# Pairing VectorE's maxima and normalisations, and two heads' value products side by side in TensorE's columns, in a transformer block on one core

## What is computed

```python
# dil: three patterns, each a band; mixed by a softmax over their log-denominators
s = einsum(q, k) * scale + bias        # bias from 32 buckets of the distance
s = where(mask, s, -inf);  m = max(s);  p = exp(s - m);  l = sum(p)
o = einsum(p / l, v)
# na: the same softmax over a window of rows and 16 columns, with its own bias
# diff: two maps per head
p = softmax(einsum(q * HD ** -0.5, k));  a = p[0] - lam * p[1];  o = einsum(a, v)
```

## Time and profile before

| | |
|---|---|
| three runs | 4605.14 (4602.17 to 4606.09) us |
| the profiled execution | 4605.48 us |
| its span, first to last instruction | 4603.7 us |
| PE busy | 3929.3 us, 85% |
| VectorE busy | 2265.8 us, 49% |
| ScalarE busy | 1411.2 us, 31% |
| mean granted TensorE clock | 0.936 of full |
| mean DMA traffic | 60 GB/s |

### The profile page before, as it was taken

The page is one execution under the profiler, slowest core; times in us unless marked ns, Lnnn a source line. Parts: engine busy times, 40 slices in busy tenths (PEclk is TensorE's granted clock), DMA queues, the critical chain, the costliest instruction groups (busy, mean ns, idle before and its releaser), DMA issues. The chain is left out here.

```text
span 4603.7 us, 56197 instructions
## 1 busy us (share of the span) xinstructions
PE 3929.3 (85%) x20557; PEld 2962.8 (64%) x20557; DVE 2265.8 (49%) x3881; ACT 1411.2 (31%) x2600; POOL 0.2 (0%) x4
## 2 busy tenths in 40 slices
PE   5987988998689998888698888976999888797888
PEld 3554667876456686666587665864667666575566
DVE  3434335553445525666524666234553666436654
ACT  2322223322223313333312444121332434314432
POOL 0000000000000000000000000000000000000000
PEclk8988999998799999999899999987999999899999
DMA  6333234542100021111021000211112111121112
GB/s 224 116 95 80 80 89 142 164 124 73 33 23 27 25 62 37 27 36 28 23 64 42 24 24 22 66 46 36 30 33 79 43 41 36 46 69 28 33 51 74
DMA packets 504246, 275.37 MB, mean 60 GB/s; under 512 B 56665, under 2 KB 489781, under 8 KB 504094
## 3 DMA queue, kind: packets, MB, share of 16 engines
q1 hardware_dynamic: 483186, 252.08, 19.5%
q10 hardware_dynamic: 20908, 21.26, 1.5%
HBM read 271.08 MB, written 10.32 MB: 61 GB/s over the span
## 5 line engine op out<-in xcount | busy, mean ns | idle before, releaser
L558 PE MATMUL ps<-h_high,w_high 128*128 128x512 f32 (+1 forms) x3512 | 1346.5, 383 | 185.1 <-DVEq L2191 128.9
L558 PE MATMUL ps<-h_low,w_high 128*128 128x512 f32 (+1 forms) x3512 | 1293.4, 368 | 0.0
L558 PE MATMUL ps<-h_high,w_low 128*128 128x512 f32 (+1 forms) x3512 | 1288.0, 367 | 0.0
L558 PEld LDWEIGHTS ps<-h_high,w_high 128*128 128x128 f32 x3512 | 682.7, 194 | 351.3 <-DVEq L2191 136.6
L554 DVE TENSOR_TENSOR w_low<-w_raw,w_high 128x1024 fp32r<-128x1024 f32 x378 | 453.6, 1200 | 625.2 <-ACT w_high L544 603.5
L558 PEld LDWEIGHTS ps<-h_low,w_high 128*128 128x128 f32 x3512 | 682.8, 194 | 107.7 <-issue 11.7
L558 PEld LDWEIGHTS ps<-h_high,w_low 128*128 128x128 f32 x3512 | 681.5, 194 | 109.3
L544 ACT ACTIVATE w_high<-w_raw 128x1024 fp32r<-128x1024 f32 x378 | 392.2, 1039 | 784.5 <-PE ps L558 604.6
L558 PE MATMUL ps<-k_high,q_high 64*128 64x256 f32 (+4 forms) x784 | 194.4, 414 | 255.7 <-ACT probs L777 215.2
L777 ACT ACTIVATE probs<-ps,neg_max 128x768 f32<-128x768 f32 (+2 forms) x368 | 288.4, 784 | 361.1 <-DVE neg_max L802 360.2
L558 PE MATMUL ps<-probsT,v 128*128 128x512 f32 (+4 forms) x800 | 338.4, 565 | 12.7 <-DVE probsT L949 6.7
(11 more groups left out here) (192 smaller groups left out, 4000.8 us busy)
## 6 DMA issues: line engine op xcount, KB each, us to landing
w_raw<-in_w_in SPq DMA_DIRECT2D x444, 256.0 KB, 3.1
y_and_merged<-in_w_mod SPq DMA_DIRECT2D x96, 256.0 KB, 3.1
w_raw<-in_w_branch SPq DMA_DIRECT2D x96, 256.0 KB, 3.0
w_raw<-in_w_up SPq DMA_DIRECT2D x88, 256.0 KB, 4.3
y_and_merged<-in_w_ada SPq DMA_DIRECT2D x64, 256.0 KB, 3.4
w_raw<-in_w_out SPq DMA_DIRECT2D x48, 256.0 KB, 3.0
w_raw<-in_w_down SPq DMA_DIRECT2D x44, 256.0 KB, 2.9
y_and_merged<-in_w_ada SPq DMA_DIRECT2D x4, 2048.0 KB, 21.1
```

Source lines behind the costliest of these rows:

```text
L558: return nc.tensor.matmul(*a, **kw)
```

## The change

dil and na join `TWIN`, so that they take swa's path for the values with 4 chunks of both heads instead of 8 of one head; dil, na and diff join `BOTH_FIRST`. In dil and na the wait of the scores is for `maxed` instead of `exped`. The late modulation moves from bank 7, which the odd chunks now use, to the last 128 columns of bank 1.

```diff
-TWIN = ("swa",)
-BOTH_FIRST = ("swa",)
+TWIN = ("dil", "na", "swa",)
+BOTH_FIRST = ("dil", "na", "diff", "swa",)
...
-    st += [Stage("units", name="dil", nn=5, items=8, chunks=8, **units), Stage("units", name="na", nn=4, items=8, chunks=8, **units)]
+    st += [Stage("units", name="dil", nn=5, items=8, chunks=4, **units), Stage("units", name="na", nn=4, items=8, chunks=4, **units)]
...
             if s["first"]:
-                for j in range(2):
-                    for c in range(4):
-                        res.append(([PF[:, j, qt, 128 * c:128 * c + 128] for qt in range(4)], VB[:, c, 64 * j:64 * j + 64],
-                                    PS[64 * j:64 * j + 64, 5 * 512:6 * 512], c == 0, c == 3))
+                for c in range(4):
+                    res.append([([PF[:, j, qt, 128 * c:128 * c + 128] for qt in range(4)], VB[:, c, 64 * j:64 * j + 64],
+                                 PS[64 * j:64 * j + 64, 5 * 512:6 * 512], c == 0, c == 3) for j in range(2)])
...
                 if group * size >= 2:
-                    key = "exped"
+                    key = "maxed" if s["first"] else "exped"
...
-                    mod_block(pe, s, i, s["nn"], e, 0 if e < 4 else 1, 7)
+                    mod_block(pe, s, i, s["nn"], e, 0 if e < 4 else 1, 1, 384)
...
-                    pe_values(pe, s, t, u, i, 0, side=late_mods(i, (1, 2)), first=1)
+                    pe_twin_values(pe, s, t, u, i, side=late_mods(i, (1, 2)))
...
-                    if s["first"] and c in (2, 4):
-                        act_mod(act, s, i, s["nn"], c // 2, 7)
+                    if c in (1, 3):
+                        act_mod(act, s, i, s["nn"], (c + 1) // 2, 1, 384)
...
-                    evac_pt(act, s, t, u, i, 0, 0, beside(i))
+                    evac_twin(act, s, t, u, i, 0, beside(i))
...
-                evac_pt(dve, s, t, u, i, 0, 1, beside)
+                if s["first"]:
+                    evac_twin(dve, s, t, u, i, 1, beside)
+                else:
+                    evac_pt(dve, s, t, u, i, 0, 1, beside)
```

More of the change, by code:

```diff
@@ L599, in mod_total, with mod_block, act_mod @@
             mm(col, MP[:, :], PICK[:, :], start=True, stop=True).then_inc(S["mod_sum"], 1)
-        def mod_block(pe, s, t, per, off, c, b):
+        def mod_block(pe, s, t, per, off, c, b, at=0):
             kk = plain_slot(s, t, per, off)
             pe_wait_plain(pe, s, t, per, off)
-            mod_parts(bank(b, 128), lambda kc: WN[:, kk, 128 * kc:128 * kc + 128], c).then_inc(s_n, 1)
-        def act_mod(act, s, t, per, off, b):
+            mod_parts(bank(b, 128, at), lambda kc: WN[:, kk, 128 * kc:128 * kc + 128], c).then_inc(s_n, 1)
+        def act_mod(act, s, t, per, off, b, at=0):
             act.wait_ge(s_n, cnt(s, "n", t, per, off + 1))
-            act.activation(MP[:, :], bank(b, 128), ACT.Copy).then_inc(S["mod_copy"], 1)
+            act.activation(MP[:, :], bank(b, 128, at), ACT.Copy).then_inc(S["mod_copy"], 1)
         def plain_slot(s, t, per, off):
@@ L1480, in step @@
                 if s["first"]:
-                    act_mod(act, s, i, s["nn"], 0, 7)
-                    evac_pt(act, s, t, u, i, 0, 0, beside(i))
+                    act_mod(act, s, i, s["nn"], 0, 1, 384)
+                    evac_twin(act, s, t, u, i, 0, beside(i))
                 else:
@@ L1490, in step @@
                     for e in range(3, s["nn"]):
-                        act_mod(act, s, i, s["nn"], e, 7)
+                        act_mod(act, s, i, s["nn"], e, 1, 384)
                 act_proj_z(act, nxt, t, u, i + 1)
@@ L1500, in epilogue @@
                 if s["first"]:
-                    act_mod(act, s, i, s["nn"], 0, 7)
-                evac_pt(act, s, t, u, i, 0, 0, beside(i))
+                    act_mod(act, s, i, s["nn"], 0, 1, 384)
+                    evac_twin(act, s, t, u, i, 0, beside(i))
+                else:
+                    evac_pt(act, s, t, u, i, 0, 0)
                 if s["first"]:
                     for e in range(3, s["nn"]):
-                        act_mod(act, s, i, s["nn"], e, 7)
+                        act_mod(act, s, i, s["nn"], e, 1, 384)
                 if name == "diff":
@@ L1575, in epilogue @@
                     return
-                evac_pt(dve, s, t, u, i, 0, 1)
+                if s["first"]:
+                    evac_twin(dve, s, t, u, i, 1)
+                else:
+                    evac_pt(dve, s, t, u, i, 0, 1)
                 dve_output(dve, s, t, u, i, 0)
```

## The result

The kernel before took 4605.61 us in the median of four runs (4602.17 to 4608.02), the changed kernel 4465.17 us in the median of four (4463.71 to 4467.61). The ratio is 0.9696, with a 95% interval of 0.9679 to 0.9713. The forecast of 4465 us was met. The profiled execution took 4464.37 us, which is 141.1 us less than the profiled one of before. The terms beneath the sum did not all come out as forecast, so what follows checks them one by one.

A forecast was written before the change was run, and what follows sets the result against it. PE alone was taken to bound the values, and a loop through VectorE and ScalarE to add to the scores. Terms summed to 144.6 us, less 4 for half rate: 140.6 off 4605.48 gives 4465 us, range 4440 to 4500.

The forecast's parts named there:

- Scores of dil and of na, the first three units: Scores in three units each: PE's waits for VectorE and ScalarE mostly go, saving 11.4 us in dil, 16.5 in na.
- the count of 16.1 us: Scores of a dil unit: VectorE's work ends at 15.3 us, or at 16.1 with PE's own pace between groups.
- Last units of dil and na: Scores without a next unit's projection: VectorE sets the pace, saving 4.5 and 6.2 us, 10.7 in all.
- the 14.3 of my sum: Scores of dil's last unit: 1.1 + 4 x 2.96 + 1.4 = 14.3 us, against 18.82 before.
- Values: Values of dil and na: paired products save 32 us over eight units, na's covered first copy 4 us; 36 together.
- the rival of late weights: Units of dil and na: shorter units still load as much, so weights come late; up to 35 us, 4500 us; chance 0.08.
- The rival drawn from them: Values of dil and na: copies pace the chunks, costing 26 us; chance 0.05, shared with pairs not overlapping.
- diff, layer 0: Scores of diff, layer 0: the second exp starts 1.3 us earlier over five intervals; net 5.9 us, times eight units 47 us.
- PE's side work: Rival in diff's scores: steps between groups cost PE as much as the shortened loop, half of 70 us goes; 4500 us; chance 0.08.
- diff, layer 1: Scores of diff, layer 1: net 2.8 us, times eight 23 us; 4 us taken off for half rate after idling before transposes.
- Slower rival: Wait for `normed` before transposes, all 24 units: VectorE's backlog idles PE and halves the clock; 4653 us; chance 0.03.
- The fourth rival: Low-clock stretches and the values behind them move to full rate, gaining 20 us more than counted; 4445 us; chance 0.12.

The follow-up runs named there:

- ninth kernel: The changed kernel with idle matmuls, results unused, between the scores of the last units of dil, na and diff; 4448.44 us, ratio 0.9660.
- seventh: The changed kernel with ten instead of four steps of PE's side work left behind the last group of scores in diff's layer 1; 4452.92 us, ratio 0.9669.
- eighth kernel: The changed kernel with 11 idle matmuls, results unused, filling PE's wait before the transposes in diff's layer 1; 4454.19 us, ratio 0.9673.

## Why the prediction was right or wrong

The gain of 141.1 us can be read off at the starts of the stages: 70.3 us arise in dil and na, 52.5 in diff of layer 0, 17.0 in diff of layer 1. The other 1.3 us are small shifts between them.

**Scores of dil and of na, the first three units: right.** 11.4 and 16.5 us were forecast. The stretches went from 20.66, 20.14 and 20.08 to 18.04, 16.18 and 16.04 us, together 10.6, and from 23.41, 24.92 and 23.69 to 17.61, 19.04 and 19.05 us, together 16.3. PE sets the pace, as the count of 16.1 us said, and na's second group kept 1.51 us.

**Last units of dil and na: the step that failed.** 10.7 us were forecast and 5.9 came (2.4 and 3.5). The step was "Nothing fills PE there, and VectorE sets the pace". The runs show that VectorE does not set it, PE's scores and VectorE's maxima take turns: with two slots in PSUM for the scores, each group takes both, and the next one starts only when both maxima are over, and at half rate a group is 1.68 + 2 x 0.85 us and a little for the semaphore, 3.5 us instead of 2.96. I had the earlier trace rows with a clock of 0.63 before me and counted PE at full rate. The ninth kernel shows it: at full rate the scores of dil's last unit take 14.60 us, near the 14.3 of my sum, and na's 17.42 against 16.5.

**Values: right in size, made up otherwise.** 36 us were forecast, and 37.5 is what dil and na gained beside the scores. Per unit dil gained 4.68 us, not 4.0. By the rows, the products give 3.85 of it (the last two stood in a row before and took 1.86 us), the transposes about 0.5, which I had priced at nothing by taking 1.16 us for eight, and the end of a wait ahead of the first product 0.3. On the 0.5 the Trainium skill, page "TensorEngine Tiling (Array Packing)", section "Key Properties", says that a change of the tiling mode drains TensorE. By that rule the trace agrees: products here use 64 columns of the array and transposes 128, and eight transposes take 1.02 us in a row and 1.16 in two lots. No run here tells a drain from another price of alternating. na's three units gained 6.0, 7.9 and 6.0 us where I had 5.3: its wait for the first copy went as forecast (1.60 us to none), and half rate in the second unit's values went too.

Against that, the passage from dil's last unit to na's first scores took 58.14 us instead of 60.32, no more than its scores became shorter. PE waits 1.17 us there for the last modulation weights, so the rival of late weights came true at this one place, and not in the units. What kept the gain of the values away is the clock, though. The seventh and the eighth kernel run the same code here with the same wait (1.19 and 1.18 us), and the stretch behind dil's last scores took 37.5 us in both, with a clock of 0.92, against 41.75 us in the changed kernel. The changed kernel, then the eighth:

```profile
228.64:270.39 41.75, 36.82 (x198) 26.18 (x198) 8.33 (x10) 8.88 (x15) 0.00 (x0) 0.81 0.51 137
```

```profile
230.56:268.08 37.52, 32.59 (x198) 23.46 (x198) 8.33 (x10) 8.88 (x15) 0.00 (x0) 0.92 0.59 156
```

So one piece of code took 4.2 us more or less by where half rate fell. Before the change the stretch took 41.50 us; the 4.0 us that I had forecast for this unit's values show in the profiles of those two kernels and not in the changed kernel's.

**Copies.** The copies (0.60 us on ScalarE, 0.69 on VectorE) stay hidden under a chunk of 2.03 us, in which PE has no wait. The rival drawn from them did not happen: that the evacuation of PSUM may become the bound (the Trainium skill, "TensorEngine Tiling (Array Packing)", "PSUM Bottleneck") does not decide here.

**diff, layer 0: too small.** 47 us were forecast and 52 came. Groups are 4.27 us apart, near the forecast 4.4, but in all seven units with side work the scores take 28.5 us, 6.7 less in the mean than before, where I took 5.9. The difference follows the clock, now 1.00 in all seven. The two units with the least half rate before (0.95) gained 5.4 us, those at 0.90 gained 6.2 to 6.9 and those at 0.86 gained 8.0. So the shorter loop alone is worth no more than 5.4 us, under my 5.9, and I had called the spells of half rate rarer; they are gone. PE's side work did not take the gain.

**diff, layer 1: both terms too small.** I expected 2.8 us per unit from the scores and a loss of 4 us in all behind them. The scores gave 3.3 us per unit, 25.8 in all, and the stage gained 17.0, so 8.8 us were lost behind them. The wait of 2.81 us, forecast at 3.1, brought the half rate in six of the seven units with side work. The last five of them paid about 1.5 us each (51.13 us from transposes to transposes against 49.61 behind a unit at full rate); the first paid 1.0 us, because its clock fell about 1 us later, behind the transposes. I had taken about half the units at some 1 us. The clock of the 5 us behind the first, the second and the third unit's wait shows it, after waits of the same 2.81 us:

```profile
3462.71:3467.71 5.00, 5.00 (x14) 2.64 (x15) 2.68 (x4) 0.60 (x1) 0.00 (x0) 0.66 0.00 0
3513.25:3518.25 5.00, 5.00 (x22) 2.99 (x23) 3.45 (x6) 1.45 (x3) 0.00 (x0) 1.00 0.00 0
3562.86:3567.86 5.00, 5.00 (x14) 3.15 (x15) 2.10 (x4) 0.60 (x1) 0.00 (x0) 0.69 0.00 0
```

In 5 us PE gets through 22 matmuls where the rate stays full and 14 where it falls. The errors in the two terms nearly cancel (19 forecast, 17.0 measured).

**Slower rival.** Its mechanism is real but small: VectorE's four normalisations do leave PE idle and do halve the clock behind it, in layer 1 of diff, at 1.0 to 1.6 us a unit. In the units with side work of dil and na the wait before the transposes is at most 0.07 us, and in layer 0, where the last items are short, 0.16. In the last units it had been there before and grew little, from 2.58 to 2.89 us in dil and na and by 0.4 to 0.6 us in diff. The fourth rival, that the clock gains more than I counted, took part: at least 1.3 us a unit in the mean of layer 0's seven, and 2 us in the values of na's second unit.

The sum was met to 0.5 us (140.6 forecast, 141.1 between the profiled executions) because 4.8 us too much in the last units, 2.0 in layer 1 and 1.0 in the scores of dil and na stood against 5.5 too little in layer 0, 1.5 in the values and the 1.3 of small shifts. The errors of the terms are 1 to 6 us; a hit nearer than that was luck.

## What to carry to other kernels

A loop through two engines is shortened by taking first what releases the other engine (both maxima before any normalisation) and by waiting for the last reader of a buffer and no later; here each alone gave about two thirds of the gain of both. When work is moved behind the last item of a stage, look at what PE does meanwhile: keep some of its side work for that gap, or fill it. And when a stretch's granted clock is low, price PE's own instructions there at their durations in that stretch before you call another engine the bound.

## What the runs showed of the hardware

Two products with results of 64x512, in the two halves of the array's columns, take 1.01 us together, and 1.87 us in one half. Work that computes nothing gained time: eleven matmuls in the 2.81 us gap of each unit of layer 1 took 11 us off the kernel. VectorE was ready no earlier than before; what the gap no longer did was halve the rate of what followed. Idling of 2.81 us was followed by half rate in six units of layer 1, 1 us later in the first than in the last five, and by full rate in one. The same code behind dil's last scores took 41.75 us in one profiled execution and 37.5 in two others, at clocks of 0.81 and 0.92. So the price of a gap is a spread, not one number, and an effect of 4 us or less is believed only at the place where it arises.
